# Expert weight loads 6 and 7 issued without waiting for the first gather, and the context sums stored before the first expert's tokens

## Chip, cores and metric

One core of one Trainium2 chip runs the whole kernel as one launch. The metric is device microseconds from launch to end; a profiled execution also gives the span from its first to its last instruction.

## What is computed

One step of a hybrid backbone over 512 latent and 128 context tokens of width 1024. A mixer (one projection, gated convolution, gated linear attention, output projection) is followed by an expert-choice mixture of experts, then a last normalisation. Everything is float32. The part that matters here:

```
def _ec_moe(h, w_router, w_gate, w_up, w_down):
    cap = EC_CAPACITY_FACTOR * T // N_EXPERTS      # 64 latent rows, 16 context rows
    probs = jax.nn.softmax((h @ w_router).astype(jnp.float32), axis=-1)
    gates, idx = lax.top_k(jnp.swapaxes(probs, 1, 2), cap)
    xs = h[bidx, idx]
    a = silu(einsum('becd,edf->becf', xs, w_gate)) * einsum('becd,edf->becf', xs, w_up)
    y = einsum('becf,efd->becd', a, w_down) * gates[..., None]
    return zeros_like(h).at[bidx, idx].add(y)
```

There are 16 experts; each has three 1024x1024 matrices, 12 MB, of which every byte is read once from HBM.

## The kernel before

The tokens are 5 tiles of 128 rows (NT = 5): tiles 0 to 3 are latent, tile 4 is context. The first phase (to about 325 us) computes the mixer. Its end overlaps the router: for each tile the new x is written into x_sb, normalised into xr and stored to a DRAM table hn (from which rows are gathered), and x itself is stored to a DRAM table sums (to which experts add their rows). Semaphores hn_out, sums_out (tiles 0 to 3) and sums_ctx (tile 4, two transfers, 512 KB and 128 KB) tell of these stores. ScalarE issues them from its own DMA queue.

Second phase, per expert: GpSimd gathers the expert's rows of hn into xs by an indirect DMA; TensorE multiplies them with gate and up matrices (latent rows at line 2349, context rows at 2326), then with down (2375 and 2384). For the first expert the 64 latent rows are gathered by themselves as soon as the latent choice is known (line 674, semaphore xs_full[0]); they are turned by TensorE (line 2300) and scaled by ScalarE (first_tokens, line 1123). The 16 context rows come by a gather of their own (gather_first, line 689), which waits until tile 4 is in hn (hn_out[0] at 48). When they are in, TensorE turns them (2300 again), VectorE scales them, and context_products (2326) starts.

The weights come in loads of 2 MB, numbered n = 6 * expert + u, u = 0 to 3 for the halves of gate and up in turn, 4 and 5 for down. Load n goes to ring slot n % 10 (TURNS = 10). SyncE issues all of them in order from one queue (load_rows, line 562; load 8 in four parts, load_part, line 570). Loads 0 to 9 fill the ring: each waits until first-phase data in its place is dead. From load 10 on, load n waits for TensorE to be done with load n - 10 (load_later): loads 10 and 11 for gu_used 1, which is the first half of the first expert's context_products. The last-written slot 9 lies over x_sb, so load 9 waits until the context sums have been read from it:

```
sp.wait_ge(xs_full[0], 16)
load_rows(6)
sp.wait_ge(x2c_ready, 2)
load_rows(7)
load_part(BY_ROWS, 3)
sp.wait_ge(job_done, job("lg4") + 1)
sp.wait_ge(sums_ctx, 32)
load_rows(9)
```

x2c_ready 2 says that GpSimd has finished x of tile 4. A wait in SyncE's program holds back everything after it.

Of the kernel before, what the change touches and what calls it, by code (L numbers as in the profile page):

```python
# [26 lines left out]
P = 128  # L27
# [4 lines left out]
NT = T // P  # L32
# [68 lines left out]
PAD = 32  # L101
# [104 lines left out]
def job(name):  # L206
    return JOBS.index(name)


def build(nc, x_prompt, x_sample, s_fwd, s_bwd, c, c_ctx, w_mod, b_mod, g_norm1, g_norm2, w_in, w_conv, b_conv,  # L210
# [3 lines left out]
    with ctx:  # L214
        def at(name, offset, shape, dt=F32):
            return nc.alloc_sbuf_tensor_at(name, shape, dt, offset=offset)

        def sem(name):
            return ctx.enter_context(nc.semaphore(name))
# [4 lines left out]
        def small(name, shape, dt=F32):  # L224
            n = 4
            for s in shape[1:]:
                n *= s
            t = at(name, const_next[0], shape, dt)
            const_next[0] += (n + 31) // 32 * 32
            assert const_next[0] <= A_P2  # L230
            return t

        x_sb = at("x_sb", A_X, [P, NT, D])
# [8 lines left out]
        rms = small("rms", [P, 6, NT])  # L242
# [49 lines left out]
        xr = at("xr", W_XR, [P, 2, D])  # L292
# [54 lines left out]
        sum_l, sum_c = sums[0:T_LAT, :], sums[T_LAT:T + PAD, :]  # L347
# [10 lines left out]
            exp_b_ready exp_mb_ready dec_ready diff_ready exp_d_ready ks_ready ksT_ready v_sb_ready xc_ready  # L358
            u_ready conv_mid conv_ready ya_ready og_act og_ready kv_ready state_step att_double att_ready o_sq o_norm
            yb_ready g1_ready g2_ready wscaled_ready rb_ready qk_third_in wo_half wo_read x2_ready h2_low h2_high lg_ready exp_ready  # L360
            smax_ready probs_ready probsT_ready selr_ready idx_ready wo4_read x2c_ready rootc_ready xs_ctx xTc_done xT_first state_out fin_state dve_chain act_chain
            pool_chain gu_used dl_done d_used xTp_done xs_lat xs_turned xT_lat xT_ctx pads_zero gul_done silu_lat silu_ctx act_l_ready
            act_c_ready aT_ready aTc_ready yl_ready yc_ready y_added sums_ctx
            left_in last_added last_ready last_sq last_sum last_root last_out tables_ready pad_ready
# [4 lines left out]
         exp_b_ready, exp_mb_ready, dec_ready, diff_ready, exp_d_ready, ks_ready, ksT_ready, v_sb_ready, xc_ready,  # L369
         u_ready, conv_mid, conv_ready, ya_ready, og_act, og_ready, kv_ready, state_step, att_double, att_ready, o_sq,  # L370
         o_norm, yb_ready, g1_ready, g2_ready, wscaled_ready, rb_ready, qk_third_in, wo_half, wo_read, x2_ready, h2_low, h2_high, lg_ready,
         exp_ready, smax_ready, probs_ready, probsT_ready, selr_ready, idx_ready, wo4_read, x2c_ready, rootc_ready, xs_ctx, xTc_done, xT_first, state_out, fin_state, dve_chain,
         act_chain, pool_chain, gu_used, dl_done, d_used, xTp_done, xs_lat, xs_turned, xT_lat, xT_ctx, pads_zero, gul_done, silu_lat, silu_ctx,
         act_l_ready, act_c_ready, aT_ready, aTc_ready, yl_ready, yc_ready, y_added, sums_ctx,
         left_in, last_added, last_ready, last_sq, last_sum, last_root, last_out, tables_ready, pad_ready,
# [10 lines left out]
        xs_full = [sem(f"xs_full{i}") for i in range(2)]  # L386
# [47 lines left out]
        def tile(t):  # L434
            return slice(t * P, (t + 1) * P)
# [16 lines left out]
        def result(eng, name):  # L452

            eng.wait_ge(job_done, job(name) + 1)
            return pairs[PAIR[name]]
# [33 lines left out]
        def _(sp):  # L489
# [66 lines left out]
            def load_rows(n):  # L556

                e, u = divmod(n, 6)
                half = u // 2 if u < 4 else u - 4
                w = (w_gate, w_up)[u % 2] if u < 4 else w_down  # L560
                src = w[0, e, half * 512:(half + 1) * 512, :]
                sp.dma_start(ring[n % TURNS].rearrange("p k n -> p (k n)"), src.rearrange("(p k) n -> p (k n)", p=P)
                             ).then_inc(w_full[n % TURNS], 16)
# [24 lines left out]
            load_rows(4)  # L588
            sp.wait_ge(job_done, job("wo4") + 1)
            load_rows(5)  # L590
            sp.wait_ge(xs_full[0], 16)
            load_rows(6)
            sp.wait_ge(x2c_ready, 2)
            load_rows(7)
            load_part(BY_ROWS, 3)
            sp.wait_ge(job_done, job("lg4") + 1)
            sp.wait_ge(sums_ctx, 32)
            load_rows(9)
            for n in range(TURNS, 6 * (E - 1)):
                load_later(n)  # L600
# [141 lines left out]
        def _(act):  # L742
            a = nc.scalar
            steps = [0]

            def link(ins):
                steps[0] += 1
                ins.then_inc(act_chain, 1)
                act.wait_ge(act_chain, steps[0])
# [308 lines left out]
            def h2_turn(t, half=0):  # L1058
                pp = result(act, f"x2T{t}")
                if t >= 2:  # L1060
                    act.wait_ge(job_done, job(f"lg{t - 2}") + 1)
                rows = slice(KC // 2 * half, KC // 2 * half + KC // 2)
                a.activation(h2T[t % 2][:, rows, :], pp[:, 512 * half:512 * half + 512].rearrange("p (k n) -> p k n", n=P),
                             ACT.Copy).then_inc((h2_low, h2_high)[half], 1)

            def router_parts(t):
                act.wait_ge(job_done, job(f"lp{t}") + 1)
                if t >= 2:
                    act.wait_ge(job_done, job(f"lg{t - 2}") + 1)
                a.activation(parts[:, t % 2, :], pairs[PAIR[f"lg{t}"]][:, 0:P], ACT.Copy).then_inc(part_ready, 1)  # L1070
# [29 lines left out]
            for v, (dst, n) in enumerate(((gate_l, 2), (gate_c, 4))):  # L1100
                pp = result(act, f"g2_{v}")
                for b in range(n):
# [4 lines left out]
            square_sum(NT - 1)  # L1107
            h2_turn(NT - 1)
            h2_turn(NT - 1, 1)
            router_parts(NT - 1)  # L1110
            act.wait_ge(rootc_ready, 2)
            link(a.activation(xr[:, 0, :].rearrange("p (h j q) -> p h j q", h=2, j=4),
                         x_sb[:, NT - 1, :].rearrange("p (h q j) -> p h j q", h=2, j=4), ACT.Copy,
                         scale=rms[:, 5, NT - 1:NT]))
            act.dma_start(hn[tile(NT - 1), :], xr[:, 0, :]).then_inc(hn_out[0], 16)
            act.wait_ge(smax_ready, 2)
            a.activation(probs[:, NT - 1, :], probs[:, NT - 1, :], ACT.Exp).then_inc(exp_ready, 1)
# [1 line left out]
            def first_tokens():  # L1119

                for kk in range(KC):
                    act.wait_ge(xTp_done, kk // 4 + 1)
                    ins = a.activation(xT[:, 0, kk, 0:CAP_L], xT_ps(kk)[:, 0:CAP_L], ACT.Identity,
                                       bias=mod[:, 3 * KC + kk, 0:1], scale=scale2[:, kk, 0:1])
                    ins.then_inc(xT_first if kk < KC - 1 else xT_lat, 1)
# [56 lines left out]
                    last_sqrt(1)  # L1182

            first_tokens()
            act.dma_start(sum_c[0:P, :], x_sb[:, NT - 1, :]).then_inc(sums_ctx, 16)
            act.dma_start(sum_c[P:P + PAD, :], x_sb[0:PAD, NT - 1, :]).then_inc(sums_ctx, 16)
            for e in range(E):
                expert(e, e)

# [1235 lines left out]
```

## Time and profile before

| | |
|---|---|
| time, median of 3 runs | 869.84 us (869.76 to 872.36) |
| time of the profiled execution | 870.74 us |
| its span | 869.0 us |
| TensorE busy | 835.3 us (96%) |
| VectorE, ScalarE, GpSimd busy | 492.3, 236.8, 63.6 us |
| moved by DMA | 272.39 MB, mean 313 GB/s |

The profiled execution's time is its span and 1.7 us around it. Busy TensorE time is an average over stages; which resource ends the waits of a stage is read from the chain of waits, and how full the 16 DMA engines were from the DMA share of a stretch (1.00 is all of them all the time).

### The profile page before, as it was taken

To read this page: it belongs to the slowest core of one execution; us is meant where nothing else is said; L and a number is where in the kernel's file an instruction comes from. 1 tells how busy PE (TensorE), PEld (TensorE's weight loads), DVE (VectorE), ACT (ScalarE), POOL (GpSimd) and SP (SyncE) were. 2 spreads that over 40 slices of the span, in tenths; PEclk is the share of its full clock that TensorE was granted. 3 is DMA by queue.
4 is the path that set the end of the run, shared out by engine and by line. 5 is a ranking of instruction groups with operands and counts; after the bars stand their busy time and mean duration, and the time that the engine had idled before them with its cause. 6 is when DMAs were issued, how large, how long until landed. Compare 5 with 4: busy or idle time off the path is not lost.

```text
span 869.0 us, 14535 instructions
## 1 busy us (share of the span) xinstructions
PE 835.3 (96%) x6053; PEld 460.2 (53%) x6053; DVE 492.3 (57%) x1193; ACT 236.8 (27%) x465; POOL 63.6 (7%) x72
## 2 busy tenths in 40 slices
PE   6999999999999999899999999999999999998994
PEld 5798899899998875333333333333333323333322
DVE  3576553858375574676465565664654644654535
ACT  6557643553352325021011011011011011011014
POOL 1000000000000012111011011001001101000023
PEclk9999999999999999999999999999999999999997
DMA  9955715442338758999999999999999999999993
GB/s 330 293 201 189 247 55 184 171 134 97 109 123 356 273 201 328 345 385 420 391 386 412 404 390 409 401 388 397 416 385 387 425 384 401 410 384 409 430 349 140
DMA packets 50325, 272.39 MB, mean 313 GB/s; under 512 B 5226, under 2 KB 14542, under 8 KB 38100
## 3 DMA queue, kind: packets, MB, share of 16 engines
q1 hardware_dynamic: 45340, 255.15, 74.7%
q0 software_dynamic: 3248, 10.88, 5.0%
q10 hardware_dynamic: 1672, 5.43, 1.6%
q8 instruction: 48, 0.79, 0.4%
q14 instruction: 17, 0.14, 0.0%
HBM read 257.95 MB, written 13.57 MB: 312 GB/s over the span
## 4 chain that ended last, share of the span: by engine, by line
PE 80%; DMA 12%; DVE 4%; issue 1%; ACT 1%; SPq 1%; POOLq 0%; POOL 0%; DVEq 0%
PE pair L2349 20%; PE pair L1964 17%; PE pair L2375 11%; PE pair L2326 11%; DMA ring<-in_w_up 10%; PE pair L2384 5%; PE pair L2202 5%; PE pair L1904 2%; PE pair L1999 2%; DMA scale_b<-in_w_mod 2%; DMA xs<-hn,first_ctx 1%; PE pair L2122 1%; PE pair L2134 1%; PE pair L2112 1%; PE pair L2130 1%
## 5 line engine op out<-in xcount | busy, mean ns | idle before, releaser
L2349 PE MATMUL pair<-ring,xT 128*64 128x512 f32 x1024 | 226.7, 598 | 7.5 <-DMA ring<-in_w_up 7.1
L2349 PEld LDWEIGHTS pair<-ring,xT 128*64 128x64 f32 x1024 | 73.8, 137 | 150.1 <-issue 149.5
L2326 PE MATMUL pair<-ring,xT 128*32 128x512 f32 x1024 | 113.4, 594 | 0.9 <-DVE xT L1743 0.9
L2375 PE MATMUL pair<-ring,aT 128*64 128x512 f32 x512 | 113.4, 595 | 0.6 <-DVE aT L1748 0.6
L1131 ACT ACTIVATE xT<-xT,mod,scale 128x64 f32<-128x64 f32 x120 | 41.4, 427 | 217.0 <-DVE xT L1748 217.0
L1748 DVE STREAM_TRANSPOSE xT<-xs 32x256 f32<-32x256 f32 x180 | 78.3, 435 | 3.0
L1748 DVE STREAM_TRANSPOSE aT<-act_l 32x128 f32<-32x128 f32 x256 | 77.5, 303 | 4.1
L2375 PEld LDWEIGHTS pair<-ring,aT 128*64 128x64 f32 x512 | 35.8, 137 | 77.6 <-issue 77.6
L1964 PE MATMUL pair<-hT_hi,w_hi 128*128 128x320 f32 x320 | 75.9, 319 | 0.0
L1782 DVE TENSOR_TENSOR act_l<-act_l,pair 128x512 f32<-128x512 f32 x16 | 11.0, 687 | 113.1 <-ACT act_l L1163 113.1
L2326 PEld LDWEIGHTS pair<-ring,xT 128*32 128x32 f32 x1024 | 31.9, 110 | 80.0 <-issue 80.0
L1964 PE MATMUL pair<-hT_lo,w_hi 128*128 128x320 f32 x320 | 73.1, 310 | 0.0
L1964 PE MATMUL pair<-hT_hi,w_lo 128*128 128x320 f32 x320 | 72.9, 309 | 0.0
L2384 PE MATMUL pair<-ring,aTc 128*32 128x256 f32 x1024 | 58.8, 381 | 0.0
L1964 PEld LDWEIGHTS pair<-hT_hi,w_hi 128*128 128x128 f32 x320 | 53.1, 188 | 5.8 <-issue 4.1
L1964 PEld LDWEIGHTS pair<-hT_lo,w_hi 128*128 128x128 f32 x320 | 53.7, 188 | 0.0
L1964 PEld LDWEIGHTS pair<-hT_hi,w_lo 128*128 128x128 f32 x320 | 53.7, 188 | 0.0
L707 POOL DMA_INDIRECT sums<-y_rows,gather_idx x15 | 21.5, 1435 | 434.5 <-DVE y_rows L1774 434.5
L2384 PEld LDWEIGHTS pair<-ring,aTc 128*32 128x32 f32 x1024 | 31.5, 110 | 32.1 <-issue 13.0
L1774 DVE SCALAR_TENSOR_TENSOR y_rows<-pair,gain,gate_l 64x512 f32<-64x512 f32 x30 | 22.5, 749 | 44.2 <-PE pair L2375 44.0
L1774 DVE SCALAR_TENSOR_TENSOR y_rows<-pair,gain,gate_c 16x256 f32<-16x256 f32 x60 | 28.9, 482 | 30.1 <-PE pair L2384 29.4
L1283 DVE TENSOR_TENSOR w_lo<-p1w,w_hi 128x1024 fp32r<-128x1024 f32 (+1 forms) x33 | 29.9, 930 | 25.2 <-ACT w_hi L811 25.0
(304 smaller groups left out, 940.4 us busy)
## 6 DMA issues: line engine op xcount, KB each, us to landing
ring<-in_w_up SPq DMA_DIRECT2D x32, 2048.0 KB, 34.7
ring<-in_w_down SPq DMA_DIRECT2D x32, 2048.0 KB, 25.2
ring<-in_w_gate SPq DMA_DIRECT2D x31, 2048.0 KB, 31.2
p1w<-in_w_mod SPq DMA_DIRECT2D x8, 2048.0 KB, 8.2
p1w<-in_w_in SPq DMA_DIRECT2D x5, 2048.0 KB, 8.1
p1w<-in_w_mod SPq DMA_DIRECT2D x7, 1024.0 KB, 11.2
x_sb<-in_x_sample SPq DMA_DIRECT2D x8, 512.0 KB, 5.8
p1w<-in_w_out SPq DMA_DIRECT2D x2, 2048.0 KB, 8.5
```

The source lines that it names most:

```text
L707: g.indirect_dma_start(sums, bass.IndirectOffsetOnAxis(ap=gather_idx[0:SLOTS, e:e + 1], axis=0), y_rows[:, :], None, compute_op=ALU.add).t ...
L1131: ins = a.activation(xT[:, k % 2, kk, 0:CAP_L], xT[:, k % 2, kk, 0:CAP_L], ACT.Identity, bias=mod[:, 3 * KC + kk, 0:1], scale=scale2[:, kk ...
L1283: v.tensor_tensor(w_lo[place][:, rows, tile(j)], p1w[place][:, rows, tile(j)], rounded(name)[:, rows, tile(j)].bitcast(F32), ALU.subtract) ...
L1748: ins = v.transpose(dst[32 * r:32 * r + 32, :, 32 * s:32 * s + 32], src[32 * s:32 * s + 32, :].rearrange("p (k r c) -> p r k c", k=n, r=4) ...
L1774: ins = v.scalar_tensor_tensor(out=y_rows[first:first + n, w * b:w * b + w], in0=ps[r, :], scalar=gain[r, kind, e:e + 1], in1=row[r, :], o ...
L1904: ins = mm(pp[g:g + 32, 0:mod_width(u)], silu_c[:, k, :], w[:, k, :], start=k < 4, stop=k >= 4)
L1964: ins = mm(pp[:, s * 512:s * 512 + HALF], w, h[:, s * HALF:(s + 1) * HALF], start=k == 0 and i == 0, stop=k == KC - 1 and i == 2)
L2202: ins = mm(pp[:, half * 512:(half + 1) * 512], y, w, start=k == 0 and i == 0, stop=k == KC - 1 and i == 2)
L2326: ins = mm(ctx_ps[32 * g:32 * g + 32, :], xt[:, 4 * half + j, CAP_L:96], w[:, j, n * 512:(n + 1) * 512], start=half == 0 and j == 0, stop= ...
L2349: ins = mm(ps[64 * n:64 * n + 64, :], xt[:, kk, 0:CAP_L], w[:, j, n * 512:(n + 1) * 512], start=kk == 0, stop=kk == KC - 1)
L2375: ins = mm(y_ps[0][r:r + 64, :], aT[:, j, 64 * fh:64 * fh + 64], wd[:, j, n * 512:(n + 1) * 512], start=fh == 0 and j == 0, stop=fh == 1 a ...
L2384: ins = mm(y_ps[1][32 * b:32 * b + 32, 0:256], aTc[:, j, 32 * fh:32 * fh + 32], down[fh][:, j, 256 * b:256 * b + 256], start=fh == 0 and j ...
```

## The change

Three edits. SyncE no longer waits for the first gather before load 6. ScalarE issues the two stores of the context sums right after its copies of tile 4 for the router, ahead of the store of tile 4 to hn, where before they followed first_tokens. And as load 9 might now be let go before xr has been made from x_sb, a semaphore xrc_read is set by that ScalarE instruction, and load 9 waits for it too.

```
@@ sync @@
             load_rows(5)
-            sp.wait_ge(xs_full[0], 16)
             load_rows(6)
...
             sp.wait_ge(sums_ctx, 32)
+            sp.wait_ge(xrc_read, 1)
             load_rows(9)
@@ scalar @@
             h2_turn(NT - 1)
             h2_turn(NT - 1, 1)
+            act.dma_start(sum_c[0:P, :], x_sb[:, NT - 1, :]).then_inc(sums_ctx, 16)
+            act.dma_start(sum_c[P:P + PAD, :], x_sb[0:PAD, NT - 1, :]).then_inc(sums_ctx, 16)
             router_parts(NT - 1)
             act.wait_ge(rootc_ready, 2)
-            link(a.activation(xr[:, 0, :].rearrange("p (h j q) -> p h j q", h=2, j=4),
+            a.activation(xr[:, 0, :].rearrange("p (h j q) -> p h j q", h=2, j=4),
                          x_sb[:, NT - 1, :].rearrange("p (h q j) -> p h j q", h=2, j=4), ACT.Copy,
-                         scale=rms[:, 5, NT - 1:NT]))
+                         scale=rms[:, 5, NT - 1:NT]).then_inc(xrc_read, 1)
+            act.wait_ge(xrc_read, 1)
             act.dma_start(hn[tile(NT - 1), :], xr[:, 0, :]).then_inc(hn_out[0], 16)
...
             first_tokens()
-            act.dma_start(sum_c[0:P, :], x_sb[:, NT - 1, :]).then_inc(sums_ctx, 16)
-            act.dma_start(sum_c[P:P + PAD, :], x_sb[0:PAD, NT - 1, :]).then_inc(sums_ctx, 16)
```

On SyncE, at the end of the ring's first filling, the difference of the two programs is this (ring_131 is the slot of load 4, and so on up to ring_136 for load 9; ring_127 is load 10; sums_back3 is the semaphore of tile 3's sums):

```order
 L562 DMA ring_131<-in_w_down 128x4096 [waits wo_half]
 L562 DMA ring_132<-in_w_down 128x4096 [waits job_done]
-L562 DMA ring_133<-in_w_gate 128x4096 [waits xs_full0]
+L562 DMA ring_133<-in_w_gate 128x4096
 L562 DMA ring_134<-in_w_up 128x4096 [waits x2c_ready]
 L570 DMA ring_135<-in_w_gate 128x1024 [waits job_done,sums_back3]
-L562 DMA ring_136<-in_w_up 128x4096 [waits sums_ctx,job_done]
+L562 DMA ring_136<-in_w_up 128x4096 [waits xrc_read,sums_ctx,job_done]
 L562 DMA ring_127<-in_w_down 128x4096 [waits gu_used]
 L562 DMA ring_128<-in_w_down 128x4096 [waits gu_used]
```

No load changes its place; load 6 loses its wait, and load 9 gets one more.

On ScalarE, from the sum of squares of tile 4 to the first expert's activation, before:

```order
L777 ACTIVATE xr,rms<-x_sb 128x1024 [waits x2c_ready]
L1063 ACTIVATE h2T_125<-pair 128x512 [waits job_done] x2
L1070 ACTIVATE parts<-pair 128x128 [waits job_done]
L1112 ACTIVATE xr<-x_sb,rms 128x1024 [waits rootc_ready]
L1115 DMA hn<-xr 128x1024 [waits act_chain]
L1117 ACTIVATE probs<-probs 128x16 [waits smax_ready]
L1123 ACTIVATE xT<-pair,mod,scale_54 128x64 [waits xTp_done] x8
L1185 DMA sums<-x_sb 128x1024
L1186 DMA sums<-x_sb 32x1024
L1163 ACT_TABLE_LOAD
```

And the same stretch of the changed program:

```order
L777 ACTIVATE xr,rms<-x_sb 128x1024 [waits x2c_ready]
L1063 ACTIVATE h2T_125<-pair 128x512 [waits job_done] x2
L1110 DMA sums<-x_sb 128x1024
L1111 DMA sums<-x_sb 32x1024
L1070 ACTIVATE parts<-pair 128x128 [waits job_done]
L1114 ACTIVATE xr<-x_sb,rms 128x1024 [waits rootc_ready]
L1118 DMA hn<-xr 128x1024 [waits xrc_read]
L1120 ACTIVATE probs<-probs 128x16 [waits smax_ready]
L1126 ACTIVATE xT<-pair,mod,scale_54 128x64 [waits xTp_done] x8
L1166 ACT_TABLE_LOAD
```

The two sums stores moved from behind the hn store and first_tokens to ahead of both, in the same DMA queue.

## Rows read from the trace of the kernel before

**Rows 1.** The page: span, and DMA share in 40 equal slices.

```profile
span 869.0 us, 14535 instructions
...
DMA  9955715442338758999999999999999999999993
```

**Rows 2.** Chain of waits, in order of time: start us, us, what.

```profile
656.31 41.42 DMA ring<-in_w_up
...
697.86 8.78 PE pair L2349 x32
...
755.82 42.80 DMA ring<-in_w_up
...
798.75 7.09 PE pair L2349 x32
```

**Rows 3.** TensorE's waits from 320 us on: us in total, times, longest.

```profile
PE pair L2349 <- DMA ring<-in_w_up: 7.1, 4, 3.0
```

**Rows 4.** Stretches: length, busy us of each engine, then TensorE clock, DMA share, GB/s.

```profile
363.00:450.00 87.00, 87.00 (x610) 29.86 (x610) 53.73 (x135) 13.72 (x37) 7.14 (x6) 1.00 1.01 399
...
650.00:750.00 100.00, 97.12 (x678) 33.46 (x676) 53.60 (x138) 11.84 (x30) 7.01 (x6) 0.98 1.01 400
...
330.00:340.00 10.00, 9.56 (x81) 6.99 (x83) 3.25 (x20) 7.24 (x14) 3.73 (x4) 1.00 0.66 227
350.00:360.00 10.00, 7.76 (x68) 2.94 (x68) 5.40 (x17) 0.60 (x1) 0.90 (x1) 1.00 0.88 300
```

**Rows 5.** SyncE's queue in order of time: start us, us, what was issued.

```profile
319.59 5.89 SPq L562 DMA_DIRECT2D ring<-in_w_down  x2
335.35 0.33 SPq L562 DMA_DIRECT2D ring<-in_w_gate  x1
...
353.39 0.33 SPq L562 DMA_DIRECT2D ring<-in_w_up  x1
358.79 0.80 SPq L562 DMA_DIRECT2D ring<-in_w_down  x2
```

**Rows 6.** Issue to landing (last number, us) of loads 0, 4, 9, 10.

```profile
ring<-in_w_gate SPq DMA_DIRECT2D x1, 2048.0 KB, 8.1
...
ring<-in_w_down SPq DMA_DIRECT2D x1, 2048.0 KB, 8.8
...
ring<-in_w_up SPq DMA_DIRECT2D x1, 2048.0 KB, 10.2
...
ring<-in_w_down SPq DMA_DIRECT2D x1, 2048.0 KB, 9.7
```

**Rows 7.** The same for gathers issued at 330.46, 354.99, 378.33 and 347.54 us.

```profile
xs<-hn,gather_idx POOLq DMA_INDIRECT x1, 4.9
...
xs<-hn,gather_idx POOLq DMA_INDIRECT x1, 8.8
...
xs<-hn,gather_idx POOLq DMA_INDIRECT x1, 13.7
...
xs<-hn,first_ctx POOLq DMA_INDIRECT x1, 6.0
```

**Rows 8.** The same for stores issued at 335.56 (hn) and 337.12 us (sums).

```profile
hn<-xr ACTq DMA_DIRECT2D x1, 512.0 KB, 11.2
...
sums<-x_sb ACTq DMA_DIRECT2D x1, 128.0 KB, 16.2
```

**Rows 9.** ScalarE in order of time: start us, us, what.

```profile
328.82 1.06 ACT L777 ACTIVATE xr<-x_sb 128x1024 f32<-128x1024 f32 x1
...
331.15 1.08 ACT L1063 ACTIVATE h2T<-pair 128x512 f32<-128x512 f32 x2 [1.18 <-PE pair L1943]
```

**Rows 10.** TensorE in order of time, with its idle time before a row in brackets.

```profile
336.00 0.71 PE L2300 MATMUL pair<-ident,xs 64*128 64x64 f32 x8
...
353.54 0.66 PE L2300 MATMUL pair<-ident,xs 16*128 16x16 f32 x8 [1.34 <-DMA xs<-hn,first_ctx]
355.10 7.07 PE L2326 MATMUL pair<-ring,xT 128*32 128x512 f32 x64 [0.90 <-DVE xT L1743]
```

More of the change, by code:

```diff
@@ L360, in build @@
             yb_ready g1_ready g2_ready wscaled_ready rb_ready qk_third_in wo_half wo_read x2_ready h2_low h2_high lg_ready exp_ready
-            smax_ready probs_ready probsT_ready selr_ready idx_ready wo4_read x2c_ready rootc_ready xs_ctx xTc_done xT_first state_out fin_state dve_chain act_chain
+            smax_ready probs_ready probsT_ready selr_ready idx_ready wo4_read x2c_ready rootc_ready xrc_read xs_ctx xTc_done xT_first state_out fin_state dve_chain act_chain
             pool_chain gu_used dl_done d_used xTp_done xs_lat xs_turned xT_lat xT_ctx pads_zero gul_done silu_lat silu_ctx act_l_ready
@@ L371, in build @@
          o_norm, yb_ready, g1_ready, g2_ready, wscaled_ready, rb_ready, qk_third_in, wo_half, wo_read, x2_ready, h2_low, h2_high, lg_ready,
-         exp_ready, smax_ready, probs_ready, probsT_ready, selr_ready, idx_ready, wo4_read, x2c_ready, rootc_ready, xs_ctx, xTc_done, xT_first, state_out, fin_state, dve_chain,
+         exp_ready, smax_ready, probs_ready, probsT_ready, selr_ready, idx_ready, wo4_read, x2c_ready, rootc_ready, xrc_read, xs_ctx, xTc_done, xT_first, state_out, fin_state, dve_chain,
          act_chain, pool_chain, gu_used, dl_done, d_used, xTp_done, xs_lat, xs_turned, xT_lat, xT_ctx, pads_zero, gul_done, silu_lat, silu_ctx,
@@ L590, in _ @@
             load_rows(5)
-            sp.wait_ge(xs_full[0], 16)
             load_rows(6)
@@ L597, in _ @@
             sp.wait_ge(sums_ctx, 32)
+            sp.wait_ge(xrc_read, 1)
             load_rows(9)
@@ L1109, in _ @@
             h2_turn(NT - 1, 1)
+            act.dma_start(sum_c[0:P, :], x_sb[:, NT - 1, :]).then_inc(sums_ctx, 16)
+            act.dma_start(sum_c[P:P + PAD, :], x_sb[0:PAD, NT - 1, :]).then_inc(sums_ctx, 16)
             router_parts(NT - 1)
             act.wait_ge(rootc_ready, 2)
-            link(a.activation(xr[:, 0, :].rearrange("p (h j q) -> p h j q", h=2, j=4),
+            a.activation(xr[:, 0, :].rearrange("p (h j q) -> p h j q", h=2, j=4),
                          x_sb[:, NT - 1, :].rearrange("p (h q j) -> p h j q", h=2, j=4), ACT.Copy,
-                         scale=rms[:, 5, NT - 1:NT]))
+                         scale=rms[:, 5, NT - 1:NT]).then_inc(xrc_read, 1)
+            act.wait_ge(xrc_read, 1)
             act.dma_start(hn[tile(NT - 1), :], xr[:, 0, :]).then_inc(hn_out[0], 16)
@@ L1184, in _ @@
             first_tokens()
-            act.dma_start(sum_c[0:P, :], x_sb[:, NT - 1, :]).then_inc(sums_ctx, 16)
-            act.dma_start(sum_c[P:P + PAD, :], x_sb[0:PAD, NT - 1, :]).then_inc(sums_ctx, 16)
             for e in range(E):
```

## The prediction

> **What bounds the kernel now.** I read the page first: TensorE is busy 96% of the span, which would make it the bound, but the DMA row stands at 9 from the 18th slice to the last but one [rows 1]. So two resources are full in the expert phase, and the question is which one ends the waits. The chain of waits answers it. It runs over TensorE up to expert 10, then passes twice over a transfer of weights that took 41 to 43 us from issue to use, the second time for load 87, which TensorE waited for until 798.75 [rows 2]. TensorE stood still for weights four times, 7.1 us in all [rows 3], and once the 32 matmuls behind such a wait took 8.78 us where 32 took 7.09 elsewhere [rows 2], another 1.7 us. So TensorE had 8.8 us to give away before load 87. From 363 us on the DMA engines had no gap: share 1.01 in both long stretches shown, at about 400 GB/s [rows 4]. A load that waits 43 us in a full queue lands when the queue has worked through what was put before it. So the end is: when load 10 and its followers get going, plus a fixed amount of transfer, plus some 70 us of TensorE and the ending behind load 87.
>
> Next, where were the DMA engines not full? From 330 to 340 us their share is 0.66 and from 350 to 360 it is 0.88 [rows 4]: 3.4 and 1.2 us, 4.6 us of their time. The first gap lies between load 5 and load 6, which SyncE issued at 335.35, the moment the first gather had landed (330.46 plus 4.9) [rows 5, 7]. The second is load 9, held until 353.39 for the sums (337.12 plus 16.2) [rows 5, 8].
>
> **The change part by part.**
>
> *The wait before load 6 goes.* Load 5 is out by 325.5 (319.59 plus 5.89) [rows 5], so load 6 goes out there. Load 7 waits for x2c_ready, which had come by 328.82, when ScalarE's instruction with the same wait starts [rows 9]. Both engines' gaps are then filled from 332 on. SyncE's later issues (part of load 8, load 9) come sooner by what waits remain.
>
> *The sums go earlier.* ScalarE can issue them once its two h2T copies are on their way, 331.2 to 332.2 [rows 9], not after 336.7. They are two issues; the three ScalarE steps behind them may start up to 1 us later, less the wait that ScalarE had there, and I put it at 0.2 us on a path that has more slack than that below. Before, the three stores of 1152 KB took from 335.56 to 353.3 (17.8 us) to land, beside loads 6, 7 and part of 8 [rows 8]. In the changed order the sums are first. They land at the latest with the whole train, 332.2 plus 17.8, 350; by their share of it nearer 346. Load 9 follows, and with 10.2 us [rows 6] it is in by 356 to 360.
>
> *What then?* Here is the step on which I rest the forecast. All ten slots are full at that point. Load 10 needs gu_used 1, that is TensorE's first half of context_products, issued before at 358.79 [rows 5]. At that time load 9 still had until 363.6 to land (353.39 plus 10.2), so the queue did not run dry. With the change it does. The 4.6 us are won ahead of load 9, and lost again in front of load 10, whose issue is set by TensorE, not by the DMA engines. What remains of a gain is that load 10 starts on empty engines. Load 10 took 9.7 us behind load 9; a load on empty engines took 8.1 (load 0) or 8.8 (load 4) [rows 6]. So if TensorE releases the slot x later than before, load 10 lands x - 1.6 to x - 0.9 later. I take the middle, x - 1.25.
>
> *How late is TensorE?* Two paths meet at the first context product.
>
> First path, the latent rows. Their gather (256 KB) had the engines nearly to itself, 4.9 us. Now loads 6 and 7 and the sums are in flight. Gathers of 80 rows took 8.8 us beside two loads (354.99) and 13.7 in the full stream behind a scatter (378.33) [rows 7]. From below: 4.9, no delay. This one is nearest to the 8.8 case: the same queue, nothing before it in GpSimd's own queue, 64 rows and not 80, but the sums beside it. I take 8.8, 3.9 us more. TensorE's turn of these rows began at 336.00, 0.65 after the landing [rows 5, 10], so TensorE moves by 3.25. At the other end of the latent products it had stood idle for 1.34 us for the context gather [rows 10]. That leaves 1.9 us.
>
> Second path, the context rows. The hn store now stands behind 640 KB in its queue. Before, it landed at 346.8 (335.56 plus 11.2) [rows 8]. From below 0 later: the sums start 4 us ahead and meet engines that have already moved most of load 6. From above: it is the last of the train and lands at 350, 3.3 later. The same loads are worked off earlier, so I take a bit over the middle, 1.9. The gather behind it took 6.0 [rows 7] and was at once waited for, so x is 1.9 by this path too.
>
> With both, x = 2.0 (from 0 to 3.3 on the second path alone).
>
> *The other pieces.* The wait on xrc_read costs nothing: xr is made by 336, load 9 is let go ten us later by sums_ctx. The link's semaphore is replaced by another. TensorE being 2 us late at 355 is hidden by the 8.8 us that it gives away later; without these it would cost 2 us. The gather for expert 2 (line 698) moves by x too and falls into the new empty stretch.
>
> *Sum.* 2.0 - 1.25 is 0.75 us later for load 10, for load 87, and for the end: 870.74 for the profiled execution becomes 871.5. The median of the runs shown lies 0.9 under the profiled one, so as a median 869.84 plus 0.75, 870.6.
>
> *A rule against the trace.* The first gather's rows show 4.9 us on nearly free engines and 8.8 in traffic [rows 7]. The Trainium skill (DMA: Bandwidth & Descriptors, Anatomy of one DMA — SWDGE (gpsimd) path) has about 2.0 us plus bytes over 436 GB/s for a GpSimd DMA, 2.6 us for this one, whatever else runs. By it the first path would move by nothing. The same page (Issuing engines are not separate DMA queues) says that all queues end on the same 16 engines and interleave. The 8.8 us agree with the second.
>
> **The rivals.**
>
> *The engines' gap is won back in full, faster.* For it: the 4.6 us are real, and the end hangs on load 87. The time would be 869.84 - 4.6 = 865.2. It decides if load 10 can be issued before load 9 has drained, that is if the first release comes 4 us earlier, for which nothing in the change provides; or if load 9 stays late. Against: the ring has only ten slots. Chance 0.13.
>
> *The first gather waits like the steady ones, slower.* With 13.7 us it is 8.8 later, TensorE 8.8 - 0.65 - 1.34 = 6.8, the end 5.55 later: 875.4. It decides from about x = 3.9, when the end passes 0.3% (2.6 us): a gather of 10.8 us. Against: the 13.7 ones stand behind a scatter of their own queue. Chance 0.18.
>
> *The gather is not delayed, about the same.* If small transfers slip between the weights, path one gives 0 and path two 0 to 1.9: the end moves by -1.25 to 0.65, middle 869.5. Against: the 8.8 row. Chance 0.14. (This is the time by the page's first rule.)
>
> *The clock, inside my own case.* TensorE would idle 3.3 us before its turn of rows. Behind the wait that ended at 697.86 its clock was down for a while (0.98 over 650 to 750) and 1.7 us went [rows 2, 4]; behind the longest one, 3.0 us [rows 3], which ended at 798.75, the matmuls took 7.09 as ever [rows 2]. If it falls here, x is 3.7 and the end 2.45 later, 872.3, just at the bound.
>
> **How the numbers follow.** The likeliest case, x near 2 and the ring running dry, has 0.55, with a range of its own from 868.5 to 873. What this measurement tells from no change is about 0.3%, 2.6 us. Faster: the first rival and a little of the third, 0.15. Slower: 0.18 and the tail of mine with the clock, 0.27. Same: 0.58. For 8 in 10 I leave out most of the faster rival below 867.0 and the worst of the slower one above 875.2.
>
> **What would show it.** Right: load 6 issued at 325 to 326, load 9 before 348; the DMA share near 1.00 from 332 to 350, then a hole of 4 to 8 us before load 10; load 10 issued at 360 to 361.5; the first gather 8 to 9.5 us to landing; the hn store landed at 348 to 349; load 87 still waited for, at 799 to 800; fewer waits for weights in all. Wrong: no hole before load 10 (then the gain is there), or TensorE's row at 355.10 coming after 359, or a chain in the second half that passes only over TensorE.

## The result, and the profile after

| | before | changed |
|---|---|---|
| median of 15 runs | 870.38 us | 873.74 us |
| profiled execution, span | 869.0 us | 872.0 us |

The ratio is 1.0038 with a 95% interval from 1.003 to 1.0046: the change costs 3.4 us, between 2.6 and 4.0. The forecast was 0.75 us slower, with a range that holds the result. The question is why the cost is more than four times that. Two executions far outside all others (935.8 us in e2, 2125.7 us in the runs of the kernel before that e9 to e12 are compared with) are left out of every ratio.

The page of the changed kernel, its DMA row beside that of before [rows 1]: the 16th slice (327 to 349 us) has risen from 8 to 9, and the 17th (349 to 371 us), the first of the expert phase, has fallen from 9 to 5.

```profile
span 872.0 us, 14535 instructions
...
DMA  9964714532348669599999999999999999999993
```

SyncE's queue of the changed kernel, in order of time (compare [rows 5]): loads 6, 7 and 9 go out 8 to 11 us earlier, and load 10, the first one that TensorE must release, 4.3 us later.

```profile
324.76 0.44 SPq L562 DMA_DIRECT2D ring<-in_w_gate  x1
327.72 0.33 SPq L562 DMA_DIRECT2D ring<-in_w_up  x1
...
343.92 0.33 SPq L562 DMA_DIRECT2D ring<-in_w_up  x1
363.12 0.95 SPq L562 DMA_DIRECT2D ring<-in_w_down  x2
```

Stretches of the changed kernel (length, busy time of each engine, TensorE clock, DMA share, GB/s): the DMA engines are full from 329 to 349, then fall idle, do nothing at all for five microseconds, and are full again behind load 10. The two gaps of before, 4.6 us of their time [rows 4], have become one. By the three stretches from 349 to 364 it is 1.25, 5.0 and 3.75 us, 10 us of their time.

```profile
329.24:339.24 10.00, 5.97 (x60) 5.42 (x60) 2.56 (x16) 3.76 (x5) 3.74 (x4) 0.95 1.00 395
339.24:349.24 10.00, 9.50 (x39) 3.49 (x41) 2.68 (x17) 3.76 (x9) 0.00 (x0) 0.71 1.01 424
349.00:354.00 5.00, 5.00 (x28) 1.76 (x26) 1.35 (x10) 0.00 (x0) 1.91 (x2) 1.00 0.75 271
354.00:359.00 5.00, 4.53 (x28) 1.62 (x24) 0.67 (x4) 0.60 (x1) 0.00 (x0) 1.00 0.00 1
359.00:364.00 5.00, 4.57 (x44) 1.76 (x48) 4.78 (x15) 0.00 (x0) 0.90 (x1) 1.00 0.25 69
...
369.00:449.00 80.00, 80.00 (x576) 27.68 (x574) 52.12 (x131) 13.42 (x36) 7.15 (x6) 1.00 1.01 403
```

TensorE of the changed kernel in order of time (compare [rows 10]): it sits idle for 4.26 us before it turns the first rows, and then eight matmuls of the first expert take 3.68 us; the same eight took 1.94 us in the kernel before (its row is shown below). By the row at 357.87 the context rows have long been there: nothing is waited for.

```profile
333.29 2.03 PE L2283 MATMUL pair<-ident 128*128 128x128 f32 x16
339.58 1.08 PE L2301 MATMUL pair<-ident,xs 64*128 64x64 f32 x8 [4.26 <-issue]
340.82 3.68 PE L2350 MATMUL pair<-ring,xT 128*64 128x512 f32 x8 [0.16 <-ACT xT L1126]
...
357.87 0.66 PE L2301 MATMUL pair<-ident,xs 16*128 16x16 f32 x8
359.43 7.07 PE L2327 MATMUL pair<-ring,xT 128*32 128x512 f32 x64 [0.90 <-DVE xT L1744]
```

The eight matmuls in the kernel before:

```profile
337.05 1.94 PE L2349 MATMUL pair<-ring,xT 128*64 128x512 f32 x8 [0.34 <-ACT xT L1123]
```

The profile puts the 4.26 us down to "issue", since it shows no releaser. What they end with is the first gather. Issue to landing (us) of the gather issued at 329.70, the hn store issued at 334.81 and load 10, of the changed kernel (before: 4.9, 11.2 and 9.7 [rows 6 to 8]):

```profile
xs<-hn,gather_idx POOLq DMA_INDIRECT x1, 9.8
...
hn<-xr ACTq DMA_DIRECT2D x1, 512.0 KB, 13.3
...
ring<-in_w_down SPq DMA_DIRECT2D x1, 2048.0 KB, 8.2
```

And the chain of waits at its end passes over load 87 as before [rows 2], 2.3 us later on a clock that started 0.8 us earlier (below):

```profile
758.89 41.98 DMA ring<-in_w_up
...
801.00 7.09 PE pair L2350 x32
```

Two executions don't start their second phase at the same microsecond: the first phase of this one was 0.76 us shorter. So I count from TensorE's turn of the chosen latent indices (below: the index turn), the step before the first gather (329.72 in the trace of before, 328.96 here). From there load 10 was issued after 29.07 us before and after 34.16 now: 5.1 us later. Load 87 was in after 468.9 and now after 471.9: 3.0 us later.

### The profile page after: what moved, and what is told of

It reads as the page before. It is cut to its first block, busy times and chain, and to the rows that moved or that the text cites. A ratio compares the mean times of both kernels' runs of the same rounds, so it can differ in the third digit from the quotient of the medians.

```text
span 872.0 us, 14535 instructions
## 1 busy us (share of the span) xinstructions
PE 835.6 (96%) x6053; PEld 459.8 (53%) x6053; DVE 493.0 (57%) x1193; ACT 236.8 (27%) x465; POOL 63.7 (7%) x72
## 4 chain that ended last, share of the span: by engine, by line
PE 80%; DMA 11%; DVE 4%; issue 2%; ACT 1%; SPq 1%; POOLq 0%; POOL 0%; DVEq 0%
PE pair L2350 21%; PE pair L1965 17%; PE pair L2376 11%; PE pair L2327 11%; DMA ring<-in_w_up 10%; PE pair L2385 5%; PE pair L2203 5%; PE pair L1905 2%; PE pair L2000 2%; DMA scale_b<-in_w_mod 1%; PE pair L2123 1%; PE pair L2135 1%; PE pair L2113 1%; PE pair L2131 1%; PE pair L1914 1%
## 5 line engine op out<-in xcount | busy, mean ns | idle before, releaser
L1775 DVE SCALAR_TENSOR_TENSOR y_rows<-pair,gain,gate_c 16x256 f32<-16x256 f32 x60 | 28.9, 482 | 30.1 <-PE pair L2385 29.4
## 6 DMA issues: line engine op xcount, KB each, us to landing
ring<-in_w_up SPq DMA_DIRECT2D x32, 2048.0 KB, 33.3
p1w<-in_w_mod SPq DMA_DIRECT2D x7, 1024.0 KB, 11.2
```

The lines of the kernel that those rows point to most:

```text
L1775: ins = v.scalar_tensor_tensor(out=y_rows[first:first + n, w * b:w * b + w], in0=ps[r, :], scalar=gain[r, kind, e:e + 1], in1=row[r, :], o ...
```

## Experiments

Theory A is the prediction's mechanism with the measured sizes: loads 6 and 7 beside the first gather double its time, TensorE idles, its clock falls, the first ring slots are released about 5 us late, and the end moves by that less the 1.5 us by which load 10 is quicker on empty engines.

**e1: only the loads.** The kernel before, without the wait ahead of load 6; the sums where they were.

```
             load_rows(5)
-            sp.wait_ge(xs_full[0], 16)
             load_rows(6)
```

> The kernel before with only the wait before load 6 taken away; the sums stay behind first_tokens. Theory A (loads 6 and 7 in flight delay the first gather, TensorE then idles, its clock falls, and the first expert's slots are released late): the first gather takes 9.0 to 9.8 us to land, TensorE turns its rows 3.5 to 4.3 us later than in the kernel before, load 10 is issued 4 to 5 us later, the DMA engines stand empty before it, and the time is 2.5 to 3.5 us above the kernel before. Theory B (the sums ahead of the gathers and of the hn store are to blame): the first gather takes 5 to 6 us and the time is that of the kernel before within 1 us.

873.23 us against 870.53, ratio 1.003 (1.0017 to 1.0043). The gather took 9.8 us and TensorE idled for 4.26 us, with the sums issued only after it:

```profile
340.58 0.85 PE L2299 MATMUL pair<-ident,xs 64*128 64x64 f32 x8 [4.26 <-issue]
341.60 3.27 PE L2348 MATMUL pair<-ring,xT 128*64 128x512 f32 x8 [0.17 <-ACT xT L1122]
```

Load 10 went out 33.3 us after the index turn. So the first edit by itself has the gather's delay, the fall of the clock and most of the time: 2.7 us of the 3.4, with intervals that overlap. Theory B is out.

**e2: only the sums.** The changed kernel with the wait put back.

```
             load_rows(5)
+            sp.wait_ge(xs_full[0], 16)
             load_rows(6)
```

> The changed kernel with the wait for the first gather before load 6 put back; only the two stores of the context sums are moved. Theory A: the first gather takes 5.0 to 5.8 us, TensorE is at most 0.5 us later, load 9 is issued by 345 us and not at 353, so the ring is full before the first release and load 10 starts on empty engines, 8.2 us to landing instead of 9.7: the time is 0 to 1.5 us below the kernel before. Theory B: the time is 2.5 to 3.5 us above it.

869.92 against 870.53 us, ratio 0.9988 (0.9973 to 1.0003): no cost, perhaps a gain. Load 9 was issued at 337.6 and not at 353, the gather took 6.7 us, load 10 went out after 28.9 us. The gather was slower than the 5.0 to 5.8 us expected. Load 9 going out 15.8 us earlier brought little or nothing, as the next load waits for TensorE. The runs were spread wide, five from 867.3 to 868.4 and six from 869.9 to 871.9; e9 to e11 come back to that.

**e3 and e12: the clock.** Unused matmuls fill TensorE's idle time in the changed kernel; e3 adds 16 pairs, e12 adds 22.

```
-            keep_warm("pTc", 8)
+            keep_warm("pTc", 24)      # e12: 30
```

> The changed kernel with 16 more pairs of the small unused matmuls by which TensorE is kept busy ahead of the first gather's rows (24 in place of 8, some 3.8 us more), so that its idle time before those rows falls from 4.3 to under 1 us; nothing else waits on them. Theory A with the clock as a part of it: the eight matmuls behind take 1.9 us again and not 3.7, the release comes 1.9 us sooner and the time is 1.5 to 2.2 us below the changed kernel. Rival (the fall of the clock is hidden behind the context gather or made up later): the time is that of the changed kernel within 0.6 us.

> The changed kernel with 22 more pairs of unused matmuls (30 in place of 8, some 5.2 us more) ahead of the first gather's rows, which cover all of TensorE's idle time there. Theory A with the clock as a part: no slow matmuls, release 1.5 to 2.0 us sooner than in the changed kernel, time 1.3 to 2.2 us below it and so 1.4 to 2.4 us above the kernel before. Rival (the clock costs nothing at the end): 3.0 to 3.8 us above the kernel before.

e3: 873.24 us, ratio 1.0028 (1.0016 to 1.004): 2.7 us above the kernel before by the medians where the changed kernel is 3.4, and by the ratios 0.9 to 1.2 us under the changed kernel (1.0038, and 1.0042 in e8). Neither expectation is met. Its gather took 10.5 us in the profiled execution, so that a wait of 1.4 us was left; the slow matmuls were gone. e12 with all of it covered: 872.44 against 870.91 us, ratio 1.0025 (1.0009 to 1.0042). TensorE of e12:

```profile
334.03 6.94 PE L2283 MATMUL pair<-ident 128*128 128x128 f32 x60
341.00 0.68 PE L2301 MATMUL pair<-ident,xs 64*128 64x64 f32 x8
342.02 1.94 PE L2350 MATMUL pair<-ring,xT 128*64 128x512 f32 x8 [0.34 <-ACT xT L1126]
```

The eight matmuls take 1.94 us again; load 10 goes out after 32.65 us, 1.5 sooner than in the changed kernel though its gather took 10.5 us and not 9.8. By the ratios e12 lies 1.1 to 1.5 us under the changed kernel, whose interval overlaps with its own. The clock's part of the release is shown. Its part of the end lies where Theory A put it, but the rival's 3.0 us above the kernel before is inside e12's interval (0.8 to 3.7 us), so that part isn't sharply measured.

**e4: one load in flight.** The wait moved from load 6 to load 7.

```
             load_rows(6)
             sp.wait_ge(x2c_ready, 2)
+            sp.wait_ge(xs_full[0], 16)
             load_rows(7)
```

> The changed kernel with the wait for the first gather put ahead of load 7: load 6 alone is in flight beside the gather. Theory A in its form one load in flight is enough (the gather's rows take turns with the load's on every engine, and load 6 has those turns to fill until 338): gather 8.5 to 9.8 us, time within 1 us of the changed kernel. Rival (the delay grows with what is queued behind): gather 6.5 to 7.5 us, time some 2 us below the changed kernel.

874.19 us (7 runs), ratio 1.0036 (1.0022 to 1.0051); the gather took 9.6 us. One 2 MB load beside the gather, with the sums' 640 KB, is as bad as two loads without them (e1). The sums alone don't do it: in e2, e6, e7, e10 and e11 they were issued beside the gather, and it took 5.1 to 6.7 us, against 4.9 to 6.3 in the kernel before, e5 and e9. A load with no store beside it wasn't run.

**e5 and e6: TensorE late, transfers untouched.** 13 unused matmul pairs ahead of the first context product, in the kernel before (e5) and in e2's kernel (e6).

```
                     claim_last(pe, 3)
+                    for _ in range(13):
+                        mm(ctx_ps[:, 0:P], ident[:, :], ident[:, :], start=True, stop=True)
```

> The kernel before with 13 unused matmul pairs (ident by ident, 3.1 us) on TensorE between its turn of the first context rows and the first context product, so that only the release of the first slots is 3 us later; no transfer is touched. Theory A (the end is set by when load 10 starts on engines that would otherwise be empty): the first 1.5 us are covered by load 9, which is still landing, the rest counts: 1.2 to 2.2 us above the kernel before. Rival C (TensorE has 8.8 us to give away, so its lateness costs nothing): within 0.5 us of the kernel before.

> The same 3.1 us of unused matmuls at the same place in the kernel that only has the sums moved (load 9 out early, ring full before the release). Theory A: the DMA engines stand empty 3.1 us longer, all of it counts: 1.2 to 2.2 us above the kernel before and 2.7 to 3.3 above the kernel without the matmuls. Rival C: as without them, 0.5 us below the kernel before.

e5: 870.32 against 870.69 us, ratio 0.9996 (0.9984 to 1.0008). e6: 869.88 us, 1.0003 (0.9986 to 1.002). By its expectation e5 has Rival C's result, and e6 lies between the two; so I had to look at what was really delayed. The matmuls take 3.17 us, but 0.9 of these lie where TensorE waited for VectorE anyway, and in e5's profiled execution the context gather, for which the kernel before had waited 1.34 us, was early: the hn store had landed in 2.8 us, not 11.2. Load 10 went out after 30.6 us, 1.5 later than before and not 3. Theory A has nothing to charge for 1.5. In e6 it went out after 30.1, 1.25 later than in e2; the ratio rose by 0.0015, 1.3 us, which is inside the noise of both. So the two experiments did not do what they were built for. They are no proof of A, but they raised a question: why was the hn store so quick?

**e7: the turn of the context rows earlier.** e2's kernel, with TensorE's turn of these rows ahead of the last eighth of the latent products.

```
                             if kk == 5:
                                 turn_choice()
+                            if kk == 7:
+                                pe.wait_ge(xT_lat, 1)
+                                pe.wait_ge(xs_ctx, 16)
+                                for c in range(KC):
+                                    ins = turn_first_rows(c, slice(CAP_L, SLOTS))
+                                ins.then_inc(xTc_done, 1)
...
-                    pe.wait_ge(xs_ctx, 16)
-                    for kk in range(KC):
-                        ins = turn_first_rows(kk, slice(CAP_L, SLOTS))
-                    ins.then_inc(xTc_done, 1)
```

> The kernel with only the sums moved, and TensorE's turn of the first context rows put ahead of the last eighth of the latent products, so that VectorE scales them meanwhile and the context products follow without the wait of 0.9 us. Theory A: load 10 is issued 0.9 us sooner and the time is 0.5 to 0.9 us below the kernel with only the sums moved, 1.0 to 2.7 us below the kernel before. Rival C: no change against the kernel with only the sums moved.

872.77 us median, ratio 1.001 (0.9992 to 1.0028), from 866.7 to 873.9: three runs under 869, the others above 871. The expectation failed for most runs. The profiled execution shows the reason. ScalarE's queue:

```profile
336.04 0.33 ACTq L1119 DMA_DIRECT2D hn<-xr  x1
```

SyncE's queue in the same trace:

```profile
335.89 0.33 SPq L562 DMA_DIRECT2D ring<-in_w_gate  x1
```

And TensorE:

```profile
354.37 0.64 PE L2302 MATMUL pair<-ident,xs 16*128 16x16 f32 x8 [3.61 <-DMA xs<-hn,first_ctx]
354.94 2.90 PE L2357 MATMUL pair<-ring,xT 128*64 128x512 f32 x8
```

Load 6 was issued 0.15 us ahead of the hn store of tile 4. The store then took 10.6 us, the context gather could start only at 347.41, and TensorE waited 3.6 us for it. Behind that wait its clock fell as well: the eight latent matmuls took 2.90 us for 1.94, the context products 7.75 for 7.07. In e2 the gather landed a little later, load 6 followed it at 336.17, and the store had gone out at 334.75: it took 3.5 us. The kernel before has the same race. In its trace the load went first by 0.2 us (335.35 and 335.56). Only one execution of e7 was traced, one of the slower ones; that its three fast executions had the store first is not shown.

**e9, e10, e11: the store always first.** One more wait ahead of load 6, for a step that ScalarE does behind its issue of the hn store; in the kernel before (e9), in e2's (e10), in e7's (e11).

```
             sp.wait_ge(xs_full[0], 16)
+            sp.wait_ge(exp_ready, 2)
             load_rows(6)
```

> The kernel before with one more wait ahead of load 6: exp_ready 2, which ScalarE sets behind its issue of the hn store of tile 4, so that this store always goes out before load 6 and not only in the executions in which the first gather lands late. Theory A: the hn store takes 2.8 to 3.5 us in every execution, the context gather is in before TensorE is through with the latent rows, its 1.34 us of idle time there go, load 10 is issued 1.0 to 1.4 us sooner; as load 9 is then still landing, 0.5 to 1.5 us below the kernel before, and its runs closer together. Rival (the order of these two makes no difference): within 0.5 us.

> The same added wait in the kernel that only has the sums moved. Theory A: all its runs fall together with the lower half of the runs without the wait, 867 to 869 us, 1.5 to 3 us below the kernel before. Rival: spread as without it, 0 to 1 us below the kernel before.

> The same added wait in the kernel with the sums moved and TensorE's turn of the first context rows ahead of the last eighth of the latent products. Theory A: the context gather has landed when TensorE comes to it (no wait of 3.6 us as in its first version), the context products follow at once, load 10 is issued 2 to 3 us sooner than in the kernel before; 866 to 868.5 us, 2 to 4 us below the kernel before. Rival: the median stays above the kernel before, as without the wait.

e9: 869.45 against 870.91 us, ratio 0.9991 (0.9976 to 1.0005). e10: 867.86 us (7 runs), 0.9969 (0.995 to 0.9989). e11: 868.58 us (12 runs), 0.9976 (0.9961 to 0.999). The hn store took 3.0 to 3.4 us in all three profiles. In each of them the first gather landed after the store had been issued (by 0.3 to 1.2 us), so this order would have come about there without the new wait. What the wait does is seen in the timed runs: nine of e7's twelve are above 871 us, and none of e11's twelve is above 870.2. e11's TensorE has no idle time up to the last context product of the first expert:

```profile
350.26 0.67 PE L2303 MATMUL pair<-ident,xs 16*128 16x16 f32 x8
350.86 1.94 PE L2358 MATMUL pair<-ring,xT 128*64 128x512 f32 x8
352.73 7.07 PE L2329 MATMUL pair<-ring,xT 128*32 128x512 f32 x64
```

e10 and e11 beat both given kernels, by 2 to 3 us against the kernel before and, by the ratios, 5 to 6 against the changed one; the two are not told apart. What the added wait does by itself is 3.0 us from e7 to e11, 1.7 us from e2 to e10 with intervals that overlap, and 0.8 us from the kernel before to e9, which is inside the noise.

**e8: the changed kernel again**, as a yardstick.

> The changed kernel once more, as the yardstick for the others of this call: 3.0 to 3.7 us above the kernel before, and with Theory A as far above it as its load 10 is issued later, less 1.5 us.

873.83 us (6 runs), ratio 1.0042 (1.0027 to 1.0057).

All profiled executions side by side, in us from the index turn, sorted by the issue of load 10, and the ratio of the timed runs:

| kernel | first gather took | hn store took | load 10 issued | load 87 in | ratio |
|---|---|---|---|---|---|
| e11 | 5.5 | 3.0 | 26.9 | 464.8 | 0.9976 |
| e9 | 5.8 | 3.0 | 28.0 | 466.5 | 0.9991 |
| e10 | 6.5 | 3.4 | 28.7 | 467.0 | 0.9969 |
| e2 | 6.7 | 3.5 | 28.9 | 466.1 | 0.9988 |
| before | 4.9 | 11.2 | 29.1 | 468.9 | |
| e6 | 5.8 | 3.0 | 30.1 | 466.5 | 1.0003 |
| e5 | 6.3 | 2.8 | 30.6 | 467.5 | 0.9996 |
| e7 | 5.1 | 10.6 | 32.2 | 469.3 | 1.001 |
| e12 | 10.5 | 13.2 | 32.7 | 468.9 | 1.0025 |
| e3 | 10.5 | 13.7 | 32.7 | 471.1 | 1.0028 |
| e4 | 9.6 | 7.2 | 33.1 | 470.6 | 1.0036 |
| e1 | 9.8 | 11.1 | 33.3 | 471.5 | 1.003 |
| changed | 9.8 | 13.3 | 34.2 | 471.9 | 1.0038 |
| e8 (changed) | 9.8 | 13.4 | 34.6 | 471.1 | 1.0042 |

From the first row to the last the issue of load 10 moves by 7.7 us and load 87 by 6.3 us. From the issue of load 10 to the landing of load 87 it is 436.2 to 438.5 us in every row but that of the kernel before, where it is 439.8. Load 9 was still landing there when load 10 went out, but so it was in e9, which has 438.5; the rest is scatter, and single rows that lie within 2 us of each other say nothing. e7 matters most here: it has no early loads and a quick gather, its load 10 is late for another reason, and its load 87 is as late as e12's. This is what e5 and e6 by themselves couldn't show: the release of the first slots sets the end.

## Why the prediction was right in kind and too small

**Where the result lies.** The slowdown clears the 2.6 us that the prediction took as the least that the measurement can tell. It is therefore the case "slower", which had 0.27, and not "same", which had 0.58; and 3.4 us above the prediction's base of 869.84 is 873.2, just past the 873 at which its central case ended. The range held it by the room kept for the slower rivals. The slower rival's condition, x above 3.9, was met, though with a gather of 9.8 us and the clock and not with one of 10.8 or more. Of the signs named, TensorE's row at 355.10 came at 359.43, past the 359 that was to count as wrong; load 10 (363.1), the first gather (9.8 us) and load 87 (801.0) lie beyond their stated limits on the late side, and the hole is 10 us of DMA time, not 4 to 8.

**The bound, and the ring running dry: right.** Load 87 ends the last wait in both traces [rows 2]; load 9 out at 343.9, before 348 as said; a hole in front of load 10; load 10 landing in 8.2 us, where 8.1 to 8.8 was taken. The gap's 4.6 us were won ahead of load 9 and lost again behind it: the rival that wins them back is out, in e2 as well, where load 10 went out no later than before.

**The price of a late release, x - 1.25: right within the scatter.** With the measured x of 5.1 it gives 3.85; load 10 landed 3.6 later (8.2 for 9.7), load 87 3.0, the median 3.4.

**"With both, x = 2.0": the step that failed, as a size.** Its first path was given 3.9 us more for the gather, and by that 3.25 for TensorE. The gather took 9.8 and not 8.8, and TensorE's first rows came 4.3 later from the index turn (10.6 after it, not 6.3). Then came the clock: 1.74 us on the eight latent matmuls and 0.2 on the turn, 2.1 up to the turn of the context rows. I had priced this at 1.7 but set it beside the central case, as one thing that could happen. It happened in the changed kernel both times it was traced, in e1 and in e4, each with 4.1 to 4.3 us idle. Less the 1.34 us of idle time, which was given back as said, this makes 4.3 + 2.1 - 1.3 = 5.1. The gather's 1.0 us and the clock's 2.1 are the whole of the miss in x.

**The second path: right, and without weight.** The hn store landed at 348.1, that is 2.1 us later from the index turn, for 1.9; but the latent products ended at 357.9, and the rows had been there before.

**The rule against the trace.** The first gather took 4.9 to 6.7 us beside little and 9.6 to 10.5 beside a load. The Trainium skill's formula for such a transfer (DMA: Bandwidth & Descriptors, Anatomy of one DMA — SWDGE (gpsimd) path) has no term for other traffic; the estimate from it was 2.6 us, and no trace here agrees with it. The 8.8 row that I went by was on the right side and still too short.

**What I had not seen in the trace of before:** that hn store and load 6 stood 0.2 us apart in two queues [rows 5, 8], and that the store took 11.2 us as the second of them, where it took 2.8 to 3.5 in the traces in which it went first. I took the 1.34 us of idle time for a fixed part of the kernel.

## What to carry to other kernels

When a stream of transfers goes round in a ring, its idle time ahead of the point at which the ring is full can be worth nothing by itself, as here: ask when the consumer gives the first slot back, and what the earlier start does to the small transfers that the consumer needs to get there. A small gather or store on which the next stage starts should go out ahead of the bulk loads, and be ordered by a wait and not by chance. Here the change that sent loads out ahead of the gather cost 3.4 us, and the two kernels in which gather and store both go first, with the sums moved, were 2 to 3 us faster than the kernel before. A delay put in to test a dependence has to be checked in the profile for how much of it arrived.

## What the runs showed of the hardware

The 512 KB store of tile 4 to hn took 2.8 to 3.5 us when it was issued 0.5 to 1.4 us ahead of the 2 MB loads of the other queue (e2, e5, e6, e9, e10, e11), and 10.6 to 11.2 when issued 0.15 to 0.2 us behind the first of them (e7, the kernel before). The 256 KB gather took 4.9 to 6.7 us without such a load issued ahead of it and 9.6 to 10.5 with one (beside the sums' stores) or with two. The single pieces in the trace of the kernel before show how store and load share the engines. Between 338 and 346 us a piece of a load (16 KB) took 0.61 us and a piece of a store (4 KB) 0.16; of 140 ends of a load's piece, 114 coincide to within 6 ns with the start of a store's piece, and of 127 ends of a store's piece, 110 with the start of a load's. So the two queues mostly take turns, piece by piece. How this adds up to the 11.2 us was not worked out.

TensorE's granted clock fell to 1.2 GHz, half of its full 2.4, behind 4.1 to 4.3 us without work (the changed kernel, e1, e4, e8), and in e7 behind 3.6 us. The stretch of the changed kernel in which it stayed at 0.50 for its whole length:

```profile
339.50:345.00 5.50, 5.26 (x19) 2.14 (x21) 0.14 (x1) 3.76 (x9) 0.00 (x0) 0.50 1.02 427
```

There eight matmuls took 3.68 us for 1.94. Behind waits of 1.0 to 1.4 us (e2, e3, e10) it did not fall. Behind waits in between it went either way. After the wait for load 87 the next 32 matmuls took 8.78 us, part of them at the lower clock, in e1, e4, e9, e10 and e11 (waits of 2.0 to 2.6 us), and 7.09 in e2, the changed kernel and the kernel before (2.0, 2.15 and 3.0 us). Only part of these 1.7 us reached the end: from the landing of load 87 to the end of the span it was 71.8 us in those five, and 71.1, 71.1 and 70.4 us in these three.
